# Moving adaLN units, two weight casts and a group norm in a two-layer decoder kernel

## The reference

```python
mod = (silu(c) @ w_ada + b_ada).reshape(B, 3, 3, D)      # shift, scale, gate of each sublayer
def sub_in(t, i):
    return rmsnorm(t, norm_pre[i]) * (1.0 + m_scale[:, i, None]) + m_shift[:, i, None]
def sub_out(t, y, i, res):
    return t + res * m_gate[:, i, None] * rmsnorm(y, norm_post[i])
x = sub_out(x, swiglu(sub_in(x, 0), ffn_up[0], ffn_down[0]), 0, FFN_RES)
h = sub_in(x, 1)
pa, pb, pg = split_cols(h @ w_in, ...)
ya, shift_new, wkv_new = rwkv7_branch(pa, ...)           # ends in a norm by groups of 64 columns
yb, conv_new, ssm_new = gdn_branch(pb, ...)              # needs inverses of unit triangular 64x64 blocks
merged = (sigmoid(g_a) * ya + sigmoid(g_b) * yb) @ w_out
x = sub_out(x, merged, 1, 1.0)
x = sub_out(x, swiglu(sub_in(x, 2), ffn_up[1], ffn_down[1]), 2, FFN_RES)
```

## Time and profile before

| | us |
|---|---|
| median of 3 runs (lowest to highest) | 2045.64 (2044.3 to 2048.57) |
| the profiled execution | 2031.48 |
| its span | 2029.7 |
| PE busy | 1896.8 (93%) |
| DVE busy | 1255.6 (62%) |
| ACT busy | 938.2 (46%) |
| transfers | 174 GB/s in the mean |

### The profile page before, as it was taken

The page is one execution under the profiler, slowest core; times in us unless marked ns, Lnnn a source line. Parts: engine busy times, 40 slices in busy tenths (PEclk is TensorE's granted clock), DMA queues, the critical chain, the costliest instruction groups (busy, mean ns, idle before and its releaser), DMA issues.

```text
span 2029.7 us, 45420 instructions
## 1 busy us (share of the span) xinstructions
PE 1896.8 (93%) x19380; PEld 1727.7 (85%) x19380; DVE 1255.6 (62%) x2186; ACT 938.2 (46%) x1834; POOL 77.6 (4%) x158
## 2 busy tenths in 40 slices
PE   5999989989999988889999999999899999789998
PEld 4999978888888877778979999798899788679997
DVE  3555356765456664878556654578654686669953
ACT  4334455444456534433444444654543764353343
POOL 0000000110000100000000000000200011000000
PEclk8999999989999988999999999999999998789999
DMA  8877765556464555698765666545544446269873
GB/s 257 246 220 223 207 172 167 165 138 165 120 186 138 162 146 146 188 285 261 215 187 166 181 178 193 156 142 151 139 113 114 128 111 166 57 157 261 252 196 108
DMA packets 556519, 353.38 MB, mean 174 GB/s; under 512 B 19620, under 2 KB 515270, under 8 KB 555022
## 3 DMA queue, kind: packets, MB, share of 16 engines
q1 hardware_dynamic: 490634, 302.74, 52.3%
q10 hardware_dynamic: 60756, 38.81, 7.2%
q0 software_dynamic: 4928, 8.92, 1.8%
HBM read 332.27 MB, written 18.50 MB: 173 GB/s over the span
## 4 chain that ended last, share of the span: by engine, by line
PE 75%; DVE 11%; DMA 5%; ACT 5%; issue 3%; POOL 1%; SPq 0%; ACTq 0%; DVEq 0%
PE bank L926 72%; DMA ring<-in_ffn_up 2%; DMA ring<-in_w_ada 2%; DVE ring_r L744 2%; PE bank L657 1%; ACT w_hi_r L736 1%; DVE far L1994 1%; PE bank L670 1%; DMA far<-t_blocks 1%; DVE big L1994 1%; DVE h L1997 1%; POOL far L638 1%; DVE big L1997 1%; DVE y L1994 1%; DVE h_r L1997 1%
## 5 line engine op out<-in xcount | busy, mean ns | idle before, releaser
L926 PE MATMUL bank<-big_r,w_hi_r 128*128 128x264 f32 x4160 | 1074.8, 293 | 48.0 <-DVE h_r L1997 23.8
L926 PE MATMUL bank<-big_r,ring_r 128*128 128x264 f32 (+1 forms) x3456 | 991.6, 287 | 0.0
L926 PEld LDWEIGHTS bank<-big_r,w_hi_r 128*128 128x128 f32 x4160 | 745.1, 190 | 110.9 <-issue 87.1
L926 PE MATMUL bank<-h_r,w_hi_r 128*128 128x264 f32 x2752 | 794.3, 289 | 0.0
L744 DVE TENSOR_TENSOR ring_r<-ring,w_hi_r 128x1024 fp32r<-128x1024 f32 (+2 forms) x440 | 523.3, 1195 | 390.3 <-ACT w_hi_r L736 386.4
L926 PEld LDWEIGHTS bank<-big_r,ring_r 128*128 128x128 f32 (+1 forms) x3456 | 659.9, 191 | 1.0
L736 ACT CAST w_hi_r<-ring 128x1024 fp32r<-128x1024 f32 (+2 forms) x440 | 452.1, 1029 | 445.9 <-PE bank L926 199.8
L926 PEld LDWEIGHTS bank<-h_r,w_hi_r 128*128 128x128 f32 x2752 | 527.1, 192 | 1.6 <-issue 0.5
L926 PE MATMUL bank<-ring,c 128*32 128x256 f32 x1152 | 94.5, 409 | 16.0 <-DMA ring<-in_w_ada 13.2
L926 PE MATMUL bank<-big,far 64*64 64x64 f32 (+2 forms) x1440 | 102.7, 253 | 0.0
L926 PEld LDWEIGHTS bank<-big,far 64*64 64x64 f32 (+1 forms) x1440 | 85.9, 138 | 9.6 <-issue 9.1
(11 more groups left out here) (304 smaller groups left out, 1949.5 us busy)
## 6 DMA issues: line engine op xcount, KB each, us to landing
ring<-in_ffn_up SPq DMA_DIRECT2D x176, 512.0 KB, 4.8
ring<-in_w_in SPq DMA_DIRECT2D x148, 512.0 KB, 3.7
ring<-in_w_ada SPq DMA_DIRECT2D x144, 512.0 KB, 4.4
ring<-in_ffn_down SPq DMA_DIRECT2D x64, 512.0 KB, 4.3
far<-in_state_gdn_ssm ACTq DMA_DIRECT2D x28, 512.0 KB, 6.3
ring<-in_ffn_down SPq DMA_DIRECT2D x32, 384.0 KB, 3.5
ring<-in_w_out SPq DMA_DIRECT2D x16, 512.0 KB, 4.8
out_sample_gdn_ssm<-far ACTq DMA_DIRECT2D x16, 512.0 KB, 5.2
```

The source lines that it names most:

```text
L926: return pe.matmul(out, lhsT, rhs, start=start, stop=stop)
```

## The change

It has five parts, none of which changes what is computed.

1. Two edges get a fourth adaLN unit: the one behind the mixing of layer 0 and the one from layer 0 into layer 1 (`edge_pieces`). The pieces behind move up: the second feed-forward of layer 0 has pieces in turns 0 to 15 and no longer in turn 16, and layer 1's first feed-forward only in turn 0, where it is the summing piece. `ring_slots` walks the longer edges accordingly.
2. Two of an edge's units stay between the means, and the rest goes behind the second mean (`edge_ends`): one unit at edges with three, two at edges with four.
3. ACT does an edge's copies behind the eight entering activations instead of behind the seventh square.
4. ACT's two casts and DVE's two subtractions for the first tiles of the second feed-forward's up product move ahead: the casts each behind the leaving activations of the last two out tiles, the subtractions ahead of DVE's wait for the first rsqrt.
5. In turns 68 and 69 DVE does the third lot's substitution behind the group norm.

The pieces of the diff stand in the order of the file: the plan, then PE, ACT and DVE.

```diff
-    if turn >= ((FT + 6, 17), (2, 0))[l][i_ffn] and not (l == 0 and i_ffn == 1 and FT < turn < FT + 6):
+    if turn >= ((FT + 6, 16), (1, 0))[l][i_ffn] and not (l == 0 and i_ffn == 1 and FT < turn < FT + 6):
...
-    return EDGE if (l, sub) in ((0, 0), (0, 1), (0, 2), (1, 0)) else 0
+    return {(0, 0): EDGE, (0, 1): EDGE + 1, (0, 2): EDGE + 1, (1, 0): EDGE}.get((l, sub), 0)
...
-    for n in edges:
-        order[n:n + EDGE + 2] = [n + EDGE, n + EDGE + 1, *range(n, n + EDGE)]
+    for n, units in edges:
+        order[n:n + units + 2] = [n + units, n + units + 1, *range(n, n + units)]
...
                     def edge_begins(sub):
-                        ada_pieces(edge_pieces(l, sub))
+                        ada_pieces(edge_pieces(l, sub) and 2)
+
+                    def edge_ends(m, sub):
+                        mean_square()
+                        ada_pieces(max(edge_pieces(m, sub) - 2, 0))
...
-                        mean_square()
+                        edge_ends(l - 1, 2)
                     ffn(0)
-                    mean_square()
+                    edge_ends(l, 0)
...
                     edge_begins(1)
-                    mean_square()
+                    edge_ends(l, 1)
                     ffn(1)
...
-                    def square_input(start=False, m=None, late=False):
+                    def square_input(start=False):
...
-                            if m and j == 6:
-                                ada_pieces(edge_pieces(*m))
                         if start:
                             ada_pieces(ADA_UNITS)
-                        for o in range(NT - 2 if late else NT, NT):
-                            ahead(act, high, (l, "out", o))
                         normalise()
...
                         enter(2 * i_ffn, hi_ffn)
+                        if l or i_ffn:
+                            ada_pieces(edge_pieces(l, 1) if i_ffn else edge_pieces(l - 1, 2))
                         act.preload_act_table_set(SILU_TANH)
...
                     enter(1, hi_in)
+                    ada_pieces(edge_pieces(l, 0))
                     act.preload_act_table_set(SIGMOID)
...
                             act.wait_ge(merged.sem, merged.at(NC + 1))
+                        if o >= NT - 2:
+                            ahead(act, high, (l, "out", o))
                         state_load(o)
...
-                        for o in range(NT - 2 if s == 2 else NT, NT):
-                            ahead(dve, low, (l, "out", o))
                         dve.wait_ge(rs_ready.sem, rs_ready.next(dve))
...
+                        for o in range(NT - 2 if s == 1 else NT, NT):
+                            ahead(dve, low, (l, "out", o))
                         dve.wait_ge(rs_ready.sem, rs_ready.next(dve))
...
-                            if run and t in SOLVE[run]:
+                            if run == 1 and t in SOLVE[run]:
                                 solve(dve, run, *SOLVE[run][t])
...
                                 group_norm(j)
+                        if t in SOLVE[2]:
+                            solve(dve, 2, *SOLVE[2][t])
```

More of the change, by code:

```diff
@@ L149, in edge @@
         if edge_pieces(l, sub):
-            edges.append(len(plan))
+            edges.append((len(plan), edge_pieces(l, sub)))
         plan.extend(units(edge_pieces(l, sub)))
@@ L1596, in _ @@
                     else:
-                        square_input(m=(l - 1, 2))
+                        square_input()
                     for m in range(0 if l else 2):
@@ L1600, in _ @@
                     ffn(0)
-                    square_input(m=(l, 0))
+                    square_input()
                     enter(1, hi_in)
+                    ada_pieces(edge_pieces(l, 0))
                     act.preload_act_table_set(SIGMOID)
@@ L1982, in _ @@
                             act.wait_ge(merged.sem, merged.at(NC + 1))
+                        if o >= NT - 2:
+                            ahead(act, high, (l, "out", o))
                         state_load(o)
                     normalise()
-                    square_input(m=(l, 1), late=True)
+                    square_input()
                     ffn(1)
```

## The result

The changed kernel takes 2046.8 us (median of 12 runs, 2043.06 to 2053.61), the kernel before, in the runs beside it, 2041.9 (2032.43 to 2048.85). The ratio is 1.0032, with a 95% interval of 1.0016 to 1.0047: slower by 6.5 us (3.3 to 9.6); the medians alone differ by 4.9. The predicted time, 2046.5, rested on a before of 2045.64 and a sum of +0.9; the forecast was no change, and the result lies outside 0.2%. So the time came out within the range, and the sum was 5.6 us too low. That 2046.5 and 2046.8 agree so closely is luck: a before that was 3.7 us too high made up for most of what the sum lacked.

The account below looks back on a forecast made before the run. TensorE was taken as the bound, three quarters of the span. The terms -1.0 - 0.1 + 0 - 0.8 - 1.9 + 1.3 + 3.4 gave +0.9 us: 2046.5 as the median, range 2039.5 to 2052.0.

Parts of the forecast that it names:

- Two casts: Edge ahead of each layer's second feed-forward: casts moved earlier hide, gaining 1.4 us in layer 0 and 0.1 in layer 1.
- The evicting copy: Edges with four units: ACT's copy ahead of the table load costs 0.4 us, but 0 at the edge into layer 1.
- The third unit at the first edge: First edge of layer 0: rsqrt starts 0.90 instead of 1.75 us behind the last squares; 0.8 gained.
- One transfer less: Layer 0's second feed-forward: one 0.52 MB load moves into ten idle microseconds; 1.9 us gained, ends 0 and 2.3.
- The sign that I had named: PE's waits for DVE's subtraction from 832 to 960 would total under 8 us.
- The edge into layer 1: Edge from layer 0 into layer 1: the fourth unit's copy hides behind the summing matmuls; cost 0.
- I take 0, because two of three units stay: All four edges: one unit less between the means may bring the lower clock, costing 0 to 1.6 us; taken as 0.
- Group norm: Turns 68 and 69, norm first: third lot's inversion 0.5 us earlier in layer 0, 1.8 later in layer 1; together +1.3.
- the landing: Third lot's last scatter lands 2.3 to 3.3 us after issue in layer 0, 3.4 in layer 1.
- The clock: Third lot's inversion: PE's standing still brings one clock fall of two, behind the longer wait; +3.4 us, ends 0 and 9.
- rival 2: The clock falls behind both third-lot inversions: +4.3 to +6.7 us, 2049.9 to 2052.3, slower; chance 0.18.
- the case at 870: Layer 0's second feed-forward: a 2.8 us wait for weights behind dense matmuls, with no clock fall (1.00).

Follow-up runs that it names:

- part 4 alone: The kernel before with only the two casts and two subtractions moved ahead: ratio 0.9995 (0.9978 to 1.0012).
- second profile of before: The unchanged kernel before, profiled once more: 2041.9 us, with a span 10.4 us longer than in its first profile.
- second run without part 5: The changed kernel with the third lot's substitution ahead of the group norm again, run a second time: 0.9982 (0.9965 to 0.9998); the first run gave 1.0000.
- moved turns: The changed kernel with the third lot's inversion one turn later: ratio 1.0016 (0.9997 to 1.0034), 2043.28 us.
- part 5 alone: The kernel before with only the group norm ahead of the third lot's substitution in turns 68 and 69: 1.0043 (1.0025 to 1.0062), 8.8 us slower.
- 36 of 54: The changed kernel with idle matmuls ahead of the third lot's inversion in both layers: with 36, ratio 1.0027; with 54, ratio 1.0004.
- two kernels: The changed kernel with 54 idle matmuls at the third lot, 1.0004; the changed kernel without part 5, with 28 and 22 at the first two lots, 0.9960.

## Why the prediction was right, and where it was wrong

**Two casts: right.** Layer 0 gained 1.44 us from the first rsqrt to the scaling, against 1.4. The changed kernel:

```profile
821.41 0.48 ACT L1516 ACTIVATE rs<-bank,epsc 128x264 f32<-128x264 f32 x1 [0.55 <-PE bank L926]
829.33 0.48 ACT L1516 ACTIVATE rs<-bank,epsc 128x264 f32<-128x264 f32 x1 [0.90 <-PE bank L926]
...
830.37 0.48 DVE L2002 SCALAR_TENSOR_TENSOR h<-xT,mod_a,rs 128x256 f32<-128x256 f32 x1 [2.14 <-ACT rs L1518]
```

The 0.90, and the scaling 1.04 behind the rsqrt, are those of the earlier trace rows. Layer 1 gained 0.4 in this profile and 0.2 in that of part 4 alone, against 0.1; the second profile of before has 0.2 of it too.

**The evicting copy: right, a little less.** It stands ahead of the table load, which starts 7.21 us behind the scaling instead of 6.95: 0.26 against 0.4.

```profile
837.21 0.35 ACT L1502 COPY ada_rows<-bank 128x256 f32<-128x256 f32 x1
837.58 1.28 ACT L1553 ACT_TABLE_LOAD   x1
```

**The third unit at the first edge: the cause was wrong.** The rsqrt now starts 0.90 behind the last squares, as forecast. But in the second profile of before it does too, with the unit still between the means, and in the second run without part 5 it is 1.75 again, with the unit behind them. It is 0.90 or 0.91 in three of four profiles with the old place and in four of ten with the new one. So the 0.85 comes and goes with the execution. It was booked as the change's gain and is chance.

**One transfer less: the mechanism was right, the size fits.** The transfers move 107 GB/s in the ten idle microseconds (829 to 839) where they moved 2; it is 106 or 107 in all ten profiles with the new order and 2 or 3 in the four with the old one. The feed-forward's stretch took 152.5 us instead of 154.3; over the executions, it was between 151.6 and 152.7 in six of ten profiles with the new order (153.6 to 156.8 in the other four), and between 154.1 and 154.9 in three of four with the old one (160.1 in the fourth). The medians differ by 1.9, as forecast, but the two groups overlap, so the size isn't shown. The sign that I had named was too coarse: PE's waits for the subtraction total 9.2 us in ten, not under 8.

```profile
PE bank L926 <- DVE ring_r L744: 9.2, 10, 1.7
```

**The edge into layer 1: forecast 0, lost up to 2.0.** The step "I take 0, because two of three units stay" failed. PE's wait ahead of the second mean grew from 1.36 to 1.79 us. In the ten profiles with two units between the means, the two stretches beside that table load take 213.0 to 215.3 us together (214.3 in the mean), in the four with three units 213.2 to 213.6 (213.3).

**Group norm: the mechanism was right, both sizes too small.** The waits of 1.06 and 2.81 went (one of 1.69 for the norm came later, at 693.43), PE ran 3.7 us ahead in layer 0, and POOL's scatters became late, as forecast. DVE's wait for ACT's factor in layer 1 is there with 1.18 us (forecast 1.2):

```profile
1675.20 0.48 DVE L2002 SCALAR_TENSOR_TENSOR big<-bank,pcol,big 128x256 f32<-128x256 f32 x1 [1.18 <-ACT big L1518]
```

But the inversions start 1.8 and 3.2 us later (703.30 - 699.05 - 2.41, and 1699.80 - 1686.97 - 9.67, with the shift of the mark ahead taken off), where I had -0.5 and +1.8: 5.0 in all against 1.3. The failed step is the landing, which I took to be the same in the new order: 3.4 us for layer 1, the median of the eight, and 2.3 to 3.3 for layer 0. After, first layer 0 and then layer 1:

```profile
L638 POOL DMA_DIRECT2D far<-t_blocks x8: 562/564/583, 695.1 to 699.0; - x8
...
DMA to landing us min/median/max: 2.8/3.6/4.5
...
L638 POOL DMA_DIRECT2D far<-t_blocks x8: 562/562/583, 1691.5 to 1695.4; - x8
...
DMA to landing us min/median/max: 2.1/2.3/4.5
```

PE needs all eight scatters, so it is the landing that comes last that counts, and that is neither the median nor the maximum of this view: the 4.5 us are the sixth scatter's in both layers, and the 4.2 of the earlier trace rows the fourth's. The eighth scatter alone, before in layer 0 and 1, then after in layer 0 and 1:

```profile
L638 POOL DMA_DIRECT2D far<-t_blocks x1: 564/564/564, 694.3 to 694.3; - x1
...
DMA to landing us min/median/max: 3.3/3.3/3.3
...
L638 POOL DMA_DIRECT2D far<-t_blocks x1: 564/564/564, 1682.7 to 1682.7; - x1
...
DMA to landing us min/median/max: 3.3/3.3/3.3
...
L638 POOL DMA_DIRECT2D far<-t_blocks x1: 562/562/562, 699.0 to 699.0; - x1
...
DMA to landing us min/median/max: 4.2/4.2/4.2
...
L638 POOL DMA_DIRECT2D far<-t_blocks x1: 562/562/562, 1695.4 to 1695.4; - x1
...
DMA to landing us min/median/max: 4.3/4.3/4.3
```

After, it lands at 703.26 and 1699.75, and PE starts at 703.30 and 1699.80, with it. Before, it landed at 697.57 and 1686.02, and PE started 1.5 and 0.95 us behind, bound by itself. So layer 1's inversion was close to its floor before the change: 0.95 us of the shift could be absorbed there, and in six of the nine profiles without part 5 PE waits 1.25 to 1.86 us for this landing already. In layer 1 the eighth scatter was issued 3.0 us later (the forecast 2.7, and 0.3 because the wait for the store ahead of the scatters was longer), its landing took 1.1 longer, and 0.9 was absorbed: the 3.2 measured. In layer 0 the store was issued 1.3 later (forecast 1.46), the landing took 0.9 longer, 1.4 were absorbed, and the store made a term that I did not have: from its issue to the first scatter it was 3.95 us after and 2.91 before (together the 1.8 measured), and in all five profiles of kernels with part 5 3.9 to 4.3 in this layer, in all nine without it 2.9 to 3.2. The store itself landed after 3.4 us instead of 2.3. What lengthens it was not tried. Nor is it shown that part 5 lengthens the eighth scatter's landing: in layer 1 it took 4.0 to 6.2 us in the five profiles with part 5 and 3.0 to 3.9 in the nine without, but in layer 0 4.1 to 4.8 and 2.3 to 5.2.

**The clock: right in kind, taken once where it came twice.** The stretch from the inversion to the table load grew by 29.9 - 25.3 = 4.6 us in layer 0 and 28.8 - 22.6 = 6.2 in layer 1. I had one fall of 3.4. Part of this rise is the good first profile: over the nine profiles without part 5 this stretch took 25.3 to 28.4 us in layer 0 and 22.6 to 27.3 in layer 1 (26.6 and 24.0 in the mean), since a fall comes there now and then in any kernel, and the inversions started 1.1 and 2.0 us earlier than in the two profiles of part 5 without idle matmuls or moved turns, not 1.8 and 3.2. By these means part 5 costs 3.1 us by the start and 7.6 by the clock, 10.7 in all, beside the 8.8 (5.1 to 12.6) of its own run. So rival 2 is what happened, at a higher price per fall. I had counted only the 9 us behind the wait, but a second fall follows behind the samples' thin matmuls (0.75 from 712.3 to 721.3 in layer 0; the kernel before had 0.81 in its own such window, 708 to 717). I had also read the case at 870 as one against a fall; that wait was 2.8 us with dense matmuls of 128x264 on both sides, whereas these waits were 5.5 us and the matmuls behind are 64x32. The Trainium skill's page "TensorE: Matmul & The Clock Gate", section "HAM oscillation — how this bites in real kernels", which says that the work behind such a wait starts cold each time, was borne out at both inversions (0.63 and 0.62).

In time, the parts come to +8.8 us (part 5 alone) and between -3.7 and 0 (the rest); the forecast had +4.7 and -3.8. So the forecast of no change rested on part 5 costing half of what it costs: the two terms that were mis-sized are the later start (+1.3) and the clock (+3.4).

## What to carry to other kernels

An order that ends a visible wait of PE can be worth less than nothing when the chain behind it is already near its floor: before moving work ahead of a chain, measure the chain from its first instruction to its consumer, with the time at which the last transfer lands and not the median or the longest landing, and compare it with an instance that did wait. What PE gains by running ahead comes back as standing still, and the standing is paid a second time in the clock of what follows. Where such a wait can't be removed, idle matmuls that fill it whole were cheaper than the wait here; two thirds of them (36 of 54) were worth nothing that the time could tell.

## What the runs showed of the hardware

The clock follows what PE did ahead. The fourteen profiles have 84 inversions. In 60 PE waited 1.79 to 5.63 us for the scatters, and the granted clock over the next 9 us was 0.50 to 0.81 in all of them. In 16 it waited less than 0.1 us, six of them behind idle matmuls (two kernels), and the clock was 1.00 in all. The eight waits of 1.09 to 1.69 us, all at the third lot, went either way: 1.00 in four, 0.62 or 0.81 in four. The first 64 matmuls alone are a poor sign: they took 2.06 us behind eight waits of 1.1 to 1.9 us at the third lot, of which four were followed by a fall within the 9 us. The clock also falls without any wait, behind sixteen matmuls of 128x8, to 0.62 in layer 1 of one run and not at all in the same place of another. Executions of one kernel differ by up to 21 us (2029.55 to 2050.9 in 35 runs of the kernel before), and such falls at places that no edit touches go with much of it: the mean granted clock of these runs was 0.952 to 0.968, lower in the longer ones (correlation -0.79). That they make all of it isn't shown: the two profiles of the kernel before differ by 10.4 us, and their mean clocks were 0.963 and 0.962.

Scatters of 32 KB, issued by POOL one behind the other at 0.56 us each, landed after 2.0 us at the least and 6.2 at the most. The page "DMA: Bandwidth & Descriptors" of the Trainium skill, section "Anatomy of one DMA — SWDGE (gpsimd) path", gives 2.0 us plus the bytes over a rate; that is the shortest here, and no plan for a series of scatters should go by it.
